# Keys and queries without norm factors, and the second inverse level as 32x32 blocks, in a hybrid gated-DeltaNet and experts block

## The reference

```
q, k, v = split(silu(conv(qkv)))              # centred conv of 5 taps
q = q * rsqrt(sum(q^2) + eps) * 128**-0.5     # l2norm
k = k * rsqrt(sum(k^2) + eps)
m = strict_lower((k*beta) @ k.T * decay)      # per chunk, head, direction
t_inv = inverse(I + m)                        # unit triangular
v_new = t_inv @ (v*beta) - (t_inv @ (k*beta*exp(gc))) @ s
o     = (q*exp(gc)) @ s + ((q @ k.T) * decay) @ v_new
s     = s*g_tot + (k*exp(g_last - gc)).T @ v_new
out   = rmsnorm(o_forward + o_backward) * gain * silu(z)
```

## Time and profile before

| | |
|---|---|
| median of 3 runs | 886.66 us (881.91 to 889.14) |
| span of the profiled execution | 885.7 us |
| total time of that execution | not given beside the span; the median above is 1.0 us more than the span |
| busy PE, PEld, DVE, ACT, POOL | 797.7, 655.4, 534.3, 426.8, 204.6 us |
| rounds, from scores to scores | 93.46, 201.32, 311.11, about 417 us; last inverse from 473.80 us |
| DVE busy from 56 to 70 us | 13.58 of 14.00 us |
| mean granted TensorE clock | 0.980 |

### The profile page before, as it was taken

One profiled execution on the slowest core, in us unless ns is written; L12 is line 12 of the kernel. 1 busy time (PEld: TensorE's weight loads), 2 busy tenths in 40 slices (PEclk: granted clock), 3 DMA queues, 4 the chain that ended last, 5 costly groups with the idle time before them and its releaser, 6 DMA issues.

```text
span 885.7 us, 16314 instructions
## 1 busy us (share of the span) xinstructions
PE 797.7 (90%) x6572; PEld 655.4 (74%) x6572; DVE 534.3 (60%) x792; ACT 426.8 (48%) x757; POOL 204.6 (23%) x364
## 2 busy tenths in 40 slices
PE   3999997999988998899877997998999999999975
PEld 1778885798767987689877876988777777687631
DVE  2488576347763476635565444768987675796243
ACT  3475653338534384344743235446656564674101
POOL 3102261013700137010360013001162222222201
PEclk9999999999999999999998999999999999999998
DMA  9968469434694346953948446954689999999993
GB/s 313 297 191 244 116 161 217 130 84 126 167 202 127 84 126 167 203 127 84 275 112 209 137 151 218 307 221 195 246 328 421 414 422 419 419 417 377 419 418 123
DMA packets 182022, 208.39 MB, mean 235 GB/s; under 512 B 50212, under 2 KB 155341, under 8 KB 169017
## 3 DMA queue, kind: packets, MB, share of 16 engines
q1 hardware_dynamic: 179833, 203.28, 70.6%
q0 software_dynamic: 2112, 4.04, 1.2%
HBM read 190.64 MB, written 20.22 MB: 238 GB/s over the span
## 4 chain that ended last, share of the span: by engine, by line
PE 59%; DVE 12%; DMA 11%; POOL 8%; ACT 4%; issue 4%; SPq 1%; POOLq 0%; ACTq 0%; DVEq 0%
PE bank L2479 57%; DMA raw<-in_w_e_dram 5%; POOL lane L951 3%; POOL lane L953 3%; PE bank L2482 2%; DVE w_lo L2164 2%; DVE chan L1814 2%; DMA problem_rows<-lane 2%; DMA lane<-problem_rows 1%; DMA raw<-in_w_ada_dram 1%; SPq L605 1%; DVE half_lo L1718 1%; ACT lane L1274 1%; DMA lane<-inverse 1%; POOL key_rs L913 1%
## 5 line engine op out<-in xcount | busy, mean ns | idle before, releaser
L2479 PE MATMUL bank<-hT,half_hi 128*128 128x256 f32 (+1 forms) x1024 | 229.0, 319 | 3.4 <-ACT z_raw L1258 2.3
L2479 PEld LDWEIGHTS bank<-hT,half_hi 128*128 128x128 f32 x1024 | 167.1, 192 | 17.9 <-issue 3.4
L2479 PE MATMUL bank<-hT,half_lo 128*128 128x256 f32 (+1 forms) x512 | 159.6, 312 | 0.0
L1718 DVE TENSOR_TENSOR half_lo<-half_raw,half_hi 128x1024 fp32r<-128x1024 f32 x88 | 108.9, 1238 | 38.7 <-ACT half_hi L1142 38.3
L2479 PE MATMUL bank<-lane 64*64 64x64 f32 (+2 forms) x2096 | 101.5, 236 | 17.2 <-issue 6.3
L2479 PEld LDWEIGHTS bank<-lane 64*64 64x64 f32 (+2 forms) x2096 | 93.0, 148 | 29.9 <-issue 18.0
L2164 DVE TENSOR_TENSOR w_lo<-raw,w_hi 128x2048 fp32r<-128x2048 f32 x36 | 85.8, 2394 | 46.7 <-ACT w_hi L1583 46.6
L1142 ACT CAST half_hi<-half_raw 128x1024 fp32r<-128x1024 f32 x88 | 91.9, 1047 | 30.4 <-PE bank L2479 23.1
L2479 PEld LDWEIGHTS bank<-hT,half_lo 128*128 128x128 f32 x512 | 98.2, 192 | 5.5
L1583 ACT CAST w_hi<-raw 128x2048 fp32r<-128x2048 f32 x36 | 68.7, 1909 | 33.5 <-DMA raw<-in_w_e_dram 16.9
L1814 DVE SCALAR_TENSOR_TENSOR chan<-bank,conv_col,chan 128x508 f32<-128x508 f32 (+3 forms) x96 | 63.1, 658 | 7.7 <-ACT chan L1211 5.2
(11 more groups left out here) (374 smaller groups left out, 1409.0 us busy)
## 6 DMA issues: line engine op xcount, KB each, us to landing
raw<-in_w_e_dram SPq DMA_DIRECT2D x96, 1024.0 KB, 11.7
half_raw<-in_w_in_dram SPq DMA_DIRECT2D x64, 512.0 KB, 5.1
half_raw<-in_w_ada_dram SPq DMA_DIRECT2D x32, 512.0 KB, 4.7
raw<-in_w_ada_dram SPq DMA_DIRECT2D x8, 1024.0 KB, 11.7
dense<-staged SPq DMA_DIRECT2D x32, 128.0 KB, 4.3
half_raw<-in_w_proj_a_dram SPq DMA_DIRECT2D x8, 512.0 KB, 5.3
half_raw<-in_w_proj_b_dram SPq DMA_DIRECT2D x8, 512.0 KB, 4.7
half_raw<-in_w_out_dram SPq DMA_DIRECT2D x8, 512.0 KB, 6.5
```

The lines of the kernel that those rows point to most:

```text
L1718: dve.tensor_tensor(half_lo[m % HBUF][:, :], half_raw[n % HRING][:, :], half_hi[m % HBUF][:, :].bitcast(F32), ALU.subtract).then_inc(s["ha ...
L2479: return nc.tensor.matmul(dst, lhsT, rhs, start=start, stop=stop)
```

## The change

Keys and queries keep their length. `silu` writes them straight to `kT` and `qT`; DVE copies the turned keys as they are to `k_nat` (`key_copy`). The squares are still summed. POOL makes the inverse roots of both keys in one go after the solve (`key_norms`) and multiplies them into the gates of each token: beta times the factor for the values, beta and beta*exp times its square for m and for the residual. What the recurrence keeps is v_new times the key's factor. The queries' factor cancels in the output norm; only the epsilon is scaled by the sum of squares (`query_norms`). `turn_back`, `back` and `normed` go.

Level 32 now works only on the four 32x32 blocks of each problem that the level fills: `quarter_p` (32 products), a plain copy of 256 columns on DVE, `quarter_up` (32 products for U, then 16 for the part of T that is read later), and negated copies in place of subtractions, half of them on ACT (`place_quarters`). It handles all problems at once and not in two halves. The mask of that level goes. `turn_channels(5)` moves from before the level's first product to after it.

```diff
-LEVELS = [16, 32]
+QUARTER = 32
...
-        TURN_AFTER = {3: ("back_copied", 2), 4: ("v_copied", 2), 5: ("k_normed", 3)}
-        BACK_AFTER = {0: ("back_copied", 0), 1: ("back_copied", 1), 2: ("k_normed", 4), 3: ("back_copied", 3)}
+        TURN_AFTER = {3: ("ksq_ready", 0), 4: ("v_copied", 2), 5: ("ksq_ready", 3)}
...
+        def quarter_at(b, side):
+
+            at_ = 64 * b + QUARTER * side
+            return slice(at_, at_ + QUARTER)
+
+        def quarter_cols(side):
+            return slice(QUARTER * side, QUARTER * side + QUARTER)
+
+        def by_quarter(b):
+            return bank[b][:, 0:2 * TILES * QUARTER].rearrange("p (m n) -> p m n", n=QUARTER)
 
...
-            def key_norm(n):
-                pool.wait_ge(s["ksq_ready"], j * 4 + (n + 1))
-                tiles = TILES if n < 2 else 2
-                own.after(pool.tensor_tensor(key_lin[:, n, 0:tiles], key_sq[:, n, 0:tiles], guard[:, 0:tiles], ALU.add))
-                pool.tensor_tensor(key_rs[:, n, 0:tiles], key_lin[:, n, 0:tiles], half_neg[:, 0:tiles], ALU.pow)\
-                    .then_inc(s["knorm_ready"], 1)
+            def key_norms():
+
+                pool.wait_ge(s["ksq_ready"], j * 4 + 2)
+                into, ours = key_gates[j % 2], slice(2 * j, 2 * j + 2)
+                size = [P, TILES, 2, DIRS]
+                own.after(pool.tensor_tensor(key_lin[:, :, :], key_sq[:, 0:2, :], guard[:, :].unsqueeze(1).to_broadcast([P, 2, TILES]),
+                                             ALU.add))
+                own.after(pool.tensor_tensor(key_rs[:, :, :], key_lin[:, :, :],
+                                             half_neg[:, 0:2 * TILES].rearrange("p (n t) -> p n t", n=2), ALU.pow))
+                norm = key_rs[:, :, :].rearrange("p n t -> p t n").unsqueeze(3).to_broadcast(size)
+                own.mark(pool.tensor_tensor(into[:, KEY_BETA], gates[:, BETA, :, ours, :], norm, ALU.mult))
+                own.after(pool.tensor_tensor(into[:, KEY2_NEG_BETA_EXP], gates[:, NEG_BETA_EXP, :, ours, :], norm, ALU.mult))
+                own.mark(pool.tensor_tensor(into[:, KEY2_BETA], into[:, KEY_BETA], norm, ALU.mult))
+                own.after(pool.tensor_tensor(into[:, KEY2_NEG_BETA_EXP], into[:, KEY2_NEG_BETA_EXP], norm, ALU.mult))
+                pool.tensor_copy(key_lin[:, 0, 0:1], key_rs[:, 0, 0:1]).then_inc(s["key_gates_ready"], 1)
+
+            def query_norms():
+
+                pool.wait_ge(s["ksq_ready"], j * 4 + 4)
+                pool.tensor_scalar(query_guard[j % 2][:, :, :], key_sq[:, 2:4, 0:LAT].rearrange("p h t -> p t h"), 4 * EPS, 4 * EPS * P,
+                                   ALU.add, ALU.mult).then_inc(s["q_guard_ready"], 1)
...
-                                              gates[:, BETA, t, 2 * i:2 * i + 2, d:d + 1].to_broadcast([P, 2, P]), ALU.mult)
+                                              key_gates[i % 2][:, KEY_BETA, t, :, d:d + 1].to_broadcast([P, 2, P]), ALU.mult)
...
-                    if k == 4 and i < PAIRS - 1:
-                        key_norm(0)
...
             def o_norm(p):
                 pool.wait_ge(s["o_squared"], p + 1)
-                own.after(pool.tensor_scalar(o_stat[:, 1, :], o_stat[:, 0, :], 4.0 / P, 4 * EPS, ALU.mult, ALU.add))
+                pool.wait_ge(s["q_guard_ready"], p + 1)
+                own.after(pool.tensor_scalar(o_stat[:, 1, :], o_stat[:, 0, :], 4.0 / P, None, ALU.mult))
+                own.after(pool.tensor_tensor(o_stat[:, 1, :], o_stat[:, 1, :], query_guard[p % 2][:, :, :].rearrange("p t h -> p (t h)"),
+                                             ALU.add))
                 pool.tensor_tensor(o_stat[:, 2, :], o_stat[:, 1, :], half_neg[:, 0:4], ALU.pow).then_inc(s["o_power"], 1)
...
-                key_norm(1)
-                key_norm(2)
-                key_norm(3)
+                key_norms()
                 step_inputs(2)
+                query_norms()
                 step_inputs(3)
...
-                if n == 3 or n == 0 and j:
-                    act.wait_ge(s["chan_turned"], j * 6 + (1 if n == 3 else -2))
+                if n == 0 and j:
+                    act.wait_ge(s["chan_turned"], j * 6 - 2)
                 if n in (1, 2) and j:
-                    act.wait_ge(s["back_turned"], j * 4 + (n - 2))
-                if n >= 4:
-                    act.wait_ge(s["chan_turned"], j * 6 + (n - 2))
+                    act.wait_ge(s["chan_ready"], j * 6 + (n - 2))
+                if n in (3, 4):
+                    act.wait_ge(s["chan_ready"], j * 6 + (n - 2))
+                if n == 5:
+                    act.wait_ge(s["chan_turned"], j * 6 + 3)
                 act.activation(chan[n % 3][:, 0:w], bank[n % 2][:, 0:w], ACT.Copy,
...
-            def back(n, key):
-
-                act.wait_ge(s["back_turned"], j * 4 + (key + 1))
-                if j >= 2:
-                    act.wait_ge(s["pair_free"], j)
-                if n < 4:
-                    dst, src = kT[j % 2][:, n, :], bank[2][:, :]
-                else:
-                    dst, src = qT[j % 2][:, n - 4, :], bank[2][:, 0:256]
-                act.mul(dst, src, 1.0 if n < 4 else P ** -0.5).then_inc(s["back_copied"], 1)
...
+            def place_quarters():
+                act.wait_ge(s["up_sum"], i * UP_SUMS + 3)
+                for d in range(DIRS):
+                    rows_, cols_ = quarter_at(d, d), quarter_cols(1 - d)
+                    own.mark(act.mul(u_half[rows_, :, d, cols_], by_quarter(7)[rows_, :, :], -1.0))
+
             def place_corners():
-                act.wait_ge(s["u_updated"], i * UPDATES + UPDATES)
+                own.settle()
...
+                into = kT[j % 2][:, n, :] if n < 2 else qT[j % 2][:, n - 4, :] if n >= 4 else chan[n % 3][:, 0:w]
+                if j >= 2 and n == 0:
+                    dve.wait_ge(s["pair_free"], j)
+                dve.scalar_tensor_tensor(out=into, in0=tanh_buf[n % 2][:, 0:w], scalar=1.0,
                                          in1=chan[n % 3][:, 0:w], op0=ALU.add, op1=ALU.mult)\
...
-            def normed(n, key):
-                dve.wait_ge(s["knorm_ready"], j * 4 + (key + 1))
-                if n < 4:
-                    dst, tiles = k_nat[j % 2][:, n, :, :], TILES
-                else:
-                    dst, tiles = chan[n % 3][:, 0:256].rearrange("p (t n) -> p t n", t=2), 2
-                dve.tensor_tensor(dst, bank[TURN_BANK[n]][:, 0:tiles * P].rearrange("p (t n) -> p t n", t=tiles),
-                                  key_rs[:, key, 0:tiles].unsqueeze(2).to_broadcast([P, tiles, P]), ALU.mult)\
-                    .then_inc(s["k_normed"], 1)
+            def key_copy(n):
+                dve.wait_ge(s["chan_turned"], j * 6 + (n + 1))
+                if j >= 2 and n == 0:
+                    dve.wait_ge(s["step_ready"], (j - 1) * TILES)
+                dve.tensor_copy(k_nat[j % 2][:, n, :, :].rearrange("p t n -> p (t n)"), bank[TURN_BANK[n]][:, :])\
+                    .then_inc(s["k_copied"], 1)
...
+                if g == 0:
+                    dve.wait_ge(s["key_gates_ready"], i + 1)
...
+            def quarter_copy():
+                dve.wait_ge(s["p_sum"], i * P_SUMS + 3)
+                dve.tensor_copy(p_quarter, by_quarter(6)).then_inc(s["p_masked"], 1)
+
+            def quarters_for_last():
+                dve.wait_ge(s["up_sum"], i * UP_SUMS + 3)
+                for d in range(DIRS):
+                    rows_, cols_ = quarter_at(1 - d, d), quarter_cols(1 - d)
+                    ins = dve.tensor_scalar(u_half[rows_, :, d, cols_], by_quarter(7)[rows_, :, :], -1.0, None, ALU.mult)
+                ins.then_inc(s["u_updated"], 1)
+                dve.wait_ge(s["up_sum"], i * UP_SUMS + 4)
+                for d in range(DIRS):
+                    rows_, cols_ = quarter_at(d, 1 - d), quarter_cols(d)
+                    ins = dve.tensor_scalar(t_half[rows_, :, d, cols_], by_quarter(5)[rows_, :, :], -1.0, None, ALU.mult)
+                ins.then_inc(s["u_updated"], 1)
 
...
-                updates(0)
-                normed(4, 2)
-                masks(1)
-                normed(5, 3)
-                updates(1)
+                updates()
+                quarter_copy()
+                quarters_for_last()
...
+                src = kT[j % 2][:, n, :] if n < 2 else qT[j % 2][:, n - 4, :] if n >= 4 else chan[n % 3]
...
-            def turn_back(n, key):
-                pe.wait_ge(s["k_normed"], j * 4 + (key + 1))
-                if key or j:
-                    kind, count = BACK_AFTER[key]
-                    pe.wait_ge(s[kind], count + j * (2 if kind == "v_copied" else 4))
-                for t in range(TILES if n < 4 else 2):
-                    src = k_nat[j % 2][:, n, t, :] if n < 4 else chan[n % 3][:, t * P:(t + 1) * P]
-                    ins = turn(bank[2][:, t * P:(t + 1) * P], src)
-                ins.then_inc(s["back_turned"], 1)
...
-                    pe.wait_ge(s["back_copied"], i * 4 + 4)
```

(42 more changed lines are left out.)

141 lines of the change are left out of this document (62 added, 79 removed).

## The result

The changed kernel takes 861.65 us (median of 4 runs, 860.55 to 862.71) against 885.69 us (4 runs, 881.91 to 889.14) for the kernel before: a ratio of 0.9736, with a 95% interval of 0.9703 to 0.977. Taken again with other kernels it was 862.44 us (860.83 to 866.13), a ratio of 0.9752 [0.9728, 0.9776].

A forecast was written before the change was run, and what follows sets the result against it. It took the solve's chain and inverse DMAs to set each round up to level 16's product, then TensorE-DVE hand-overs to last_p; terms -1.8 -3.8 -1.9 -2.85 -5.15 -1.0 +0.3 +0.8 sum to -15.4, giving 871.3 us, range 863 to 882.

The forecast's parts named there:

- main case: Whole kernel: 15.4 us gained, to 871.3 us; chance 0.56 (faster by over 1%).
- 31 ns for a counted 32x32 instruction: Level 32: price taken for each 32x32 instruction, from the 64x64 row, nearest in size and alternation between array parts.
- lower bound of 16 ns: Level 32: half of 31 ns per 32x32 instruction if width decides; about 8 us less in all.
- Rival (a): Solve's chain isn't shorter, and new products stall for instructions (about 1.5 us): gain 10.1 us, 876.6 us; chance 0.17.
- The prologue: Before the first scores: without the queries' last turns and copies, dense(2) starts and ends earlier, -1.8 us.
- The solve: POOL's 16x16 solve: the key's norm inside it goes, 1.27 us in each of 3 rounds, -3.8 us.
- The turn of the query and the hand-overs: Level 32, three rounds: query's turn moved behind the product, -1.9 us; one copy between product and level_up, -2.85 us.
- The fourth pair: Level 32 there: branch_a's products fill the hand-overs, so only 32 fewer instructions at 31 ns count, -1.0 us.
- The clock: Level 16's first product runs at half clock after idling in all rounds: +0.4 us in two rounds, +0.8 us.
- rival (b): Half clock reaches on into level_up(0), 3.3 us in three rounds: gain 5.5 us, 881.2 us; chance 0.09.
- Rival (c): Experts' stage, waiting for weights, hides the gain; a third passes, 881.5 us; chance 0.08.
- Rival (d): Level 32: 32x32 products don't run side by side, 132 ns each, slower at about 936 us; chance 0.05.

The follow-up runs named there:

- the run that sets it back to 31 ns: Changed kernel with the 32x32 loops turned so that eight products follow each other on one part of the array: 873.27 us, ratio 0.9855.
- the repetition: The changed kernel measured again, unaltered, beside other kernels of a later set: 862.44 us (5 runs).
- the kernel with late loads: Changed kernel, but SP starts each round's four w_in loads only when quarter_up's last product is done: 855.84 us, ratio 0.969.
- The run with work before the product: Changed kernel plus 11 identity products on TensorE before each loop round's first product of level 16: 874.66 us, ratio 0.989.
- the kernel shifted by 24: Changed kernel plus 12 identity products (24 counted instructions) in TensorE's first idle time: 870.76 us, ratio 0.9835.

## Why the prediction was right or wrong

**The direction and the mechanisms hold; a size was off.** The forecast's main case was right in its places (the first product earlier, the hand-overs shorter, the solve's end moved), and the gain was 24.0 and not 15.4 us. The total is nearer than the terms were: one cost was taken 11.7 us too high, and a wait that stood in no term took some 5 us back.

**The failed term: 31 ns for a counted 32x32 instruction.** I took the nearest row's pitch, that of 64x64 blocks, for their pattern on the array. In this kernel's order, which changes the part of the array with every product, it is 12.7 ns; with one part at a time it is 29 at full clock and 31 on average. For 640 instructions that is 11.7 us more than forecast, and the run that sets it back to 31 ns costs 9 to 11 us. It was the lower bound of 16 ns that lay near, and even it was too high. The prediction also priced that bound wrongly: 15 ns less for 640 instructions is 9.6 us and not "about 8", which would have given 861.7 us. The Trainium skill ("TensorEngine Tiling (Array Packing)", Instruction Overhead) has an overhead of about 60 cycles for each matmul, so that a narrow one takes no less time, an estimate of 25 ns at 2.4 GHz. For a counted instruction the trace is near that with one part at a time (29 ns) and does not agree for blocks that alternate between parts (12.7 ns); for a whole product of two counted instructions it would agree there, with 25.4 ns.

**What was given back: a wait that no step named.** The denser stretch outruns its own instructions. The forecast had -9.1 us for the three stretches from product to scores. With 12.7 ns in place of 31 for their 480 instructions it becomes -17.9, and -12.3 was measured in the first profile, -14.4 in the repetition. The stops behind `last_p`, 4.8 us in the one and 4.3 in the other, are of the size of what is missing: up to `last_p` the three rounds gained 18.9 us, and behind it they lost 6.6 in the one and 4.6 in the other. Rival (a) had put 1.5 us on "stalls for instructions", in the right place but as a lump without a mechanism.

**The prologue**: -2.9 for -1.8 in this profile. The repetition has 91.8 us to the scores, -1.7; executions differ here by more than the term's error. **The solve**: -1.0, -1.3, -1.3 for -1.27 each: right, and the run with the norm put back shows that it is on the path.

**The turn of the query and the hand-overs**: right in place. Product's end to `quarter_up` is 154.65 to 155.25, 0.6 us, for the forecast 0.65. From there to `last_p` it is 2.1 us for 4.0; the whole difference is the blocks' pitch (96 in 1.23 us where 3.0 were taken), and `last_p` wasn't held by DVE.

**The fourth pair**: -1.0 was forecast for its 32 instructions; its first product to `last_p` fell from 25.9 to 22.5 us, -3.4. With 12.7 ns for 160 blocks in place of 31 ns for 192 it would be 3.9. The last column as a whole fell by 5.4 us (3.1 in the repetition); no run shows where the other 2.0 us come from.

**The clock**: the first product ran at the lower clock, 3.7 us for its 64 instructions, as forecast, and rival (b), that this reaches on, is in the first round half true: 147.58 to 152.10 had 0.84. But the first product's clock cost little: in the kernel with late loads it took 2.08, 3.34 and 3.68 us in the three rounds, and these took 48.4, 48.5 and 48.6 us from product to scores. The run with work before the product doesn't price the clock, because it also moved the stops. Where the clock did cost was behind stops, in the kernel shifted by 24. Why round one's product was at the higher clock in the fastest kernel (64 in 2.1 us) I didn't follow.

**Rival (c)**, a gain hidden in the experts' stage: didn't happen: the last column of the table, which holds that stage, falls too. **Rival (d)** was wrong in sign: the blocks run side by side better than those of twice the size. The range ended at 863 because its lower end came from 16 ns, priced at 8 us, with no gain in the other terms.

**Left open**: when a packet of instructions is asked for, which decides how far ahead of an edge the loads must be away; and whether the late loads also gain something outside the stretches that I measured.

## What to carry to other kernels

Small products are paid twice, in the engine's time and in instructions; where a stretch of them gets faster, look in the profile for the queue "instruction", divide the packets by the stretch, and keep bulk loads from starting just before its packets. When a harmless edit costs several microseconds, compare where the stops without a releaser lie, counted in instructions, before believing that the edit did it; a shift of a whole packet is the control. And two changes that each uncover what the other removes must be costed together: 5 and 5 us alone were 24 together, though a part of that can lie in the place of the stops.

## What the runs showed of the hardware

- Float32 32x32 products that change the part of the array each time take 12.7 ns for each counted instruction (640 in 8.1 us), and 29 ns at full clock when eight in a row stay on one part (96 in 2.74 us; with a stretch at the lower clock 640 in 20.0 us, 31 ns).
- TensorE's instructions come in packets of 256, 128 counted matmuls with their weight loads (1536 instructions, 6 packets). In a dense stretch packets follow at 3.4 to 3.9 us, and at 5.2 to 6.7 us where 2 MB of weights started in between. A stop at the edge of a packet ends 2.3 to 2.9 us after the packet has started (46 stops in thirteen traces).
- The place of an instruction in that stream is worth 8.3 us in this kernel: 24 instructions in idle time cost that, 128 cost nothing. In the profiles 2.8 us of it are longer stops, and 5.7 us the same work at a lower granted clock after them (0.91 for 1.00 in the first round).
- 22 instructions a round in front of such a stretch kept TensorE's clock at 2.4 GHz, and 64 instructions went from 3.68 to 2.08 us, but the stops moved and grew. In the kernel with late loads, rounds whose first product took 2.08 and 3.68 us differ by 0.2 us.
